# Three edits in a two-layer hybrid decoder step: order of the sample and mixing steps, and the last norm

## The chip, the core and the metric

The kernel runs on one core of a Trainium2 chip. The core has TensorE (PE: matrix products, with its weight loads shown apart as PEld), VectorE (DVE), ScalarE (ACT), GpSimd (POOL) and SyncE (SP), which here only issues DMAs. The time is the device time of one execution in microseconds; lower is better. PE's clock is granted by the chip: a granted clock of 1.00 is 2.4 GHz, and the share shown for a stretch (PEclk) mixes that level with the one of 1.2 GHz.

## The reference

One inference step of a decoder trunk with two layers, for one prompt of 1024 tokens and eight samples of eight tokens (1088 rows of 1024 columns in all):

```python
def layer(x, past_kv, win_prev, wkv_prev, shift_prev, conv_prev, p):
    xn = rms_norm(x, p['norm_mix'])
    proj = xn @ p['w_in']
    ...
    o_nsa = nsa_attention(q, gates, kv_all, win_ext, p['cmp_pe'], p['cmp_w1'], p['cmp_w2'])
    o_rw, wkv_new, shift_new = rwkv_mixer(p_rw, shift_prev, wkv_prev, p)
    x = x + jnp.concatenate([o_nsa, o_rw], axis=-1) @ p['w_out']
    f, conv_new = conv_ffn(rms_norm(x, p['norm_ffn']), conv_prev, p)
    return x + f, ...
```

`nsa_attention` has three branches for 8 query heads and 2 key heads: compressed blocks of keys, the 8 blocks of 64 keys with the highest compressed scores ("selected"), and a sliding window of 256; sigmoid gates weigh and add the three. `rwkv_mixer` is a delta-rule recurrence over the tokens with 8 heads of 64, followed by a group norm, a bonus term and a gate. After the last layer `rms_norm(x, norm_final)` gives the outputs; `rms_norm` divides each row by the root of its mean square plus 1e-6 and multiplies by a gain per column.

## The kernel before

Activations lie transposed: 128 of the 1024 columns on the partitions, the 1088 tokens along the free axis. Each layer runs four stages, one after the other:

- `projections`, 0 to 377 us (layer 0) and 2130 to 2499 (layer 1);
- `scan_with_samples`, 377 to 918 and 2499 to 3041: the RWKV recurrence of the prompt, with the attention of the eight samples laid between its steps;
- `prompt_mixing`, 918 to 1241 and 3041 to 3369: the prompt's attention and the end of the RWKV branch;
- `dense_layer`, 1241 to 2130 and 3369 to 4282: output projection, ConvFFN and, in the last layer, the final norm.

Inside a stage each engine has generators of steps, written out by hand: `scan_tensor` beside `sample_tensor` on PE, `scan_vector` beside `sample_vector` on DVE, and so on. One function interleaves them alike on every engine, so the program order is fixed, and semaphores alone tie the engines together; an engine that waits holds up everything behind it in its own order.

**Scan stage.** `turns()` (L877) takes one scan step, then a sample step when its share is due. There are 152 scan steps, 19 for each pair of chunks of 64 tokens: Gram products, their masked turn, the start values, then five times a "y" step (L1284, 32 records of products in the trace) and a "z" step (L1297 and L1298, 64 records; L1298 alone in the last of the five), then "p" (L1306), "u" (L1313) and "state" (L1320, L1329, L1330) steps for both chunks. The products' results are added on DVE (L1430 for y and z, L1442 for the state). There are 143 sample steps, 16 for each of eight groups (one sample each) and a short closing group. On PE a group goes: the hidden layer of the key compression (L1504, in eight half-products of eight records each, one step each), scores, the importance product L1561 with the transposes of the compressed and window weights, then the products of window and compressed values ("w_out", L1571 to L1578), then the transposes of the selected weights:

```python
m.then_inc(w_out, 1)
yield
pe.wait_ge(s_exp, c + 1)
for n in range(8):
    pe.transpose(ps[:, BA + n * 64:BA + n * 64 + 64], s_[:, n * P:(n + 1) * P], ...)
```

(L1583), and the product with the selected values (L1591). In the same steps DVE ranks the 17 blocks (`block_ranks`, L1864 to L1872), masks the scores by the choice (L1743 to L1746), and finds the row maximum (to L1749); ACT then takes the exponential (L1648), which sets s_exp. A product c_made closes each group's compressed keys, and the last scan step's output is what the first RWKV loads of the next stage (ro_ga, waited for at L2340) come after.

**Mixing stage.** `blend()` (L1963) interleaves three generators on every engine: `compressed` (56 steps, seven per tile of 128 queries), `output` (the RWKV branch's group norm, bonus and gate, 43 steps) and `attention` (87 steps over 80 pieces of up to four key tiles). In each of its 87 rounds it takes a compressed step (two in the first six), then an output step when due, then the attention step. On DVE an attention step masks the scores of piece i+4 (L2162, L2165) and then forms the factors of a finished row of pieces i+2 ("scale", the reciprocal L2180 and the gate L2182, 128x2 each). On POOL `norm` (L2199) multiplies the exponentials by those factors, and PE transposes them (L2089) in the step after. POOL's compressed steps are the subtraction of the maximum (L2284), the gating `cm_sg` (L2290, asked for by PE's transposes L2221) and the counts (L2296, L2299); its output steps are `weigh(j)`: four operations of 128x512 on one token tile (L2455, L2457, L2458, L2459), all in one step, every third output step.

**Last norm.** At the end of `dense_layer` of the last layer DVE has the sums of squares per column-group in `rs` (128 x 1088). `sums()` (L2610) multiplies them by a matrix of ones, so every partition gets the sum of each token; `factor()` scales the 1088 sums (L2698), ACT takes the root (L2670) and DVE the reciprocal (L2701), all on 128x1088; eight multiplications (L2735) and their stores end the kernel.

## Time and profile before

| | us |
|---|---|
| median of three runs | 4283.41 (4283.08 to 4290.14) |
| the profiled execution | 4283.59 |
| its span in the trace | 4281.8 |
| PE busy | 3987.7 |
| DVE, POOL, ACT busy | 2198.1, 1785.7, 1121.3 |

The profile is of one execution. "Busy" is the time with an instruction of that engine running; a row that ends in [3.29 <-ACT sa_s L1648] says that the engine had been idle for 3.29 us and that the write of sa_s at L1648 ended it. PEclk is the granted clock of PE, as a share of the full one. The time of the profiled execution is 1.8 us above its span and 0.2 us from the median.

### The profile page before, as it was taken

The numbers are of one execution on the slowest core, as the hardware profiler recorded it, in microseconds if no ns is written. First come the engines' busy times: TensorE is split into PE (matmuls) and PEld (weight loads), VectorE is DVE, ScalarE is ACT, GpSimd is POOL, SyncE is SP. The second block draws the span as 40 slices with busy tenths as digits, with TensorE's granted clock in tenths as the row PEclk, the third lists the DMA queues.
The fourth block names the chain that finished last, engine by engine and source line by source line (L and its number), as shares of the span: only waits on it lengthen the run. The fifth ranks groups of instructions, "written<-read, shape, count | busy, mean of one in ns | idle before, by whom it ended". The sixth has DMA issues, their size and how long they took to land. (4 is left out here: it accounts for less than half of the span.)

```text
span 4281.8 us, 89487 instructions
## 1 busy us (share of the span) xinstructions
PE 3987.7 (93%) x37002; PEld 3633.0 (85%) x37002; DVE 2198.1 (51%) x4923; ACT 1121.3 (26%) x2467; POOL 1785.7 (42%) x2332
## 2 busy tenths in 40 slices
PE   8998999978899999999999979999888999999997
PEld 8987888865579999999899868888655799999996
DVE  6686444458754423414456864434587445244153
ACT  3153232326551100000212523233355410000011
POOL 5532212127765444434355322122377644344342
PEclk9999999979999999999999999999799999999998
DMA  3254323220012122131323452232200221311312
GB/s 132 91 158 163 97 72 81 67 90 6 12 54 104 45 96 77 45 125 46 112 85 117 135 176 76 67 79 66 90 9 10 75 92 45 108 66 45 129 40 89
DMA packets 201960, 350.42 MB, mean 82 GB/s; under 512 B 72930, under 2 KB 135650, under 8 KB 200418
## 3 DMA queue, kind: packets, MB, share of 16 engines
q1 hardware_dynamic: 201554, 344.70, 25.5%
q8 instruction: 293, 4.80, 0.5%
q14 instruction: 113, 0.93, 0.1%
HBM read 253.44 MB, written 95.90 MB: 82 GB/s over the span
## 5 line engine op out<-in xcount | busy, mean ns | idle before, releaser
L2601 POOL CAST wr_hi<-wr_raw 128x256 fp32r<-128x256 f32 x584 | 264.7, 453 | 902.8 <-PE ps L2636 897.1
L2603 POOL TENSOR_TENSOR wr_lo<-wr_raw,wr_hi 128x256 fp32r<-128x256 f32 x584 | 548.4, 939 | 46.8
L2636 PE MATMUL ps<-xh,wr_hi 128*128 128x384 f32 x2064 | 453.4, 328 | 0.0
L2636 PE MATMUL ps<-xl,wr_hi 128*128 128x384 f32 x2064 | 453.1, 327 | 0.0
L2636 PE MATMUL ps<-xh,wr_lo 128*128 128x384 f32 x2064 | 453.1, 327 | 0.0
L1377 POOL TENSOR_TENSOR rc_CT<-rc_AT,rc_masks 128x256 f32<-128x256 f32 x192 | 138.4, 741 | 665.1 <-DVE rc_AT L1412 486.4
L2636 PEld LDWEIGHTS ps<-xh,wr_hi 128*128 128x128 f32 x2064 | 349.2, 188 | 0.3
L2636 PEld LDWEIGHTS ps<-xh,wr_lo 128*128 128x128 f32 x2064 | 348.8, 188 | 0.0
L2636 PEld LDWEIGHTS ps<-xl,wr_hi 128*128 128x128 f32 x2064 | 348.7, 188 | 0.0
L2674 ACT ACTIVATE de_c<-de_c 128x1088 f32<-128x1088 f32 (+1 forms) x44 | 49.1, 1115 | 1098.4 <-DVE de_c L2761 1098.4
L2636 PE MATMUL ps<-de_mixh,wr_hi 128*128 128x384 f32 (+3 forms) x1440 | 320.8, 331 | 7.9 <-DVE de_mixl L2708 7.9
L2636 PE MATMUL ps<-de_mixl,wr_hi 128*128 128x384 f32 (+3 forms) x1440 | 318.4, 329 | 0.0
L2636 PE MATMUL ps<-de_mixh,wr_lo 128*128 128x384 f32 (+3 forms) x1440 | 317.4, 329 | 0.0
L2199 POOL TENSOR_TENSOR at_s<-at_s,at_fac 128x384 f32<-128x384 f32 (+3 forms) x320 | 256.2, 827 | 139.8 <-DVE at_fac L2182 139.0
L2722 DVE TENSOR_TENSOR de_x<-de_x,ps 128x384 f32<-128x384 f32 x168 | 79.3, 528 | 454.0 <-PE ps L2636 454.0
L1504 PE MATMUL ps<-sa_kt,cp_w 128*128 128x126 f32 x2304 | 295.2, 281 | 0.0
L1504 PEld LDWEIGHTS ps<-sa_kt,cp_w 128*128 128x128 f32 x2304 | 268.0, 191 | 9.7
L2636 PEld LDWEIGHTS ps<-de_mixh,wr_hi 128*128 128x128 f32 (+1 forms) x1440 | 245.4, 189 | 14.9 <-issue 14.9
L2636 PEld LDWEIGHTS ps<-de_mixh,wr_lo 128*128 128x128 f32 (+1 forms) x1440 | 247.4, 188 | 0.0
L2636 PEld LDWEIGHTS ps<-de_mixl,wr_hi 128*128 128x128 f32 (+1 forms) x1440 | 243.5, 188 | 0.0
L520 PE MATMUL ps<-pr_wh,xh 128*128 128x256 f32 (+1 forms) x720 | 215.7, 300 | 2.7 <-ACT pr_rsm L696 2.7
L520 PE MATMUL ps<-pr_wl,xh 128*128 128x256 f32 (+1 forms) x720 | 207.8, 289 | 0.0
(450 smaller groups left out, 8359.4 us busy)
## 6 DMA issues: line engine op xcount, KB each, us to landing
sa_kvp<-in_cache SPq DMA_DIRECT2D x128, 256.0 KB
scr_xres<-de_x SPq DMA_DIRECT2D x56, 544.0 KB, 2.7
de_x<-scr_xres SPq DMA_DIRECT2D x56, 544.0 KB, 3.6
wr_raw<-in_w_gate SPq DMA_DIRECT2D x42, 512.0 KB, 3.5
wr_raw<-in_w_up SPq DMA_DIRECT2D x42, 512.0 KB, 3.5
rc_arbk<-scr_arbk SPq DMA_DIRECT2D x32, 512.0 KB, 4.8
wr_raw<-in_w_down SPq DMA_DIRECT2D x32, 512.0 KB, 3.6
pr_raw<-in_w_rw SPq DMA_DIRECT2D x28, 512.0 KB, 4.3
```

Source lines behind the costliest of these rows:

```text
L520: mm = pe.matmul(ps[0:m, b:b + w], x[:, k, t * P:t * P + m], weights(y, i)[:, k, :], start=(k == 0 and j == 0), stop=(k == KD - 1 and j == 2))
L1377: pool.tensor_tensor(CT[:, n % 2, s], AT[:, s], mid(lev[:, n * CH:(n + 1) * CH], 4), ALU.mult).then_inc(ct_ready[s], 1)
L1504: m = pe.matmul(ps[:, b:b + 126], w1[:, kv, q, half * P:(half + 1) * P], kt[:, 2 * kv:2 * kv + 2, q % 8, q // 8:q // 8 + 63], start=(q == ...
L2199: pool.tensor_tensor(x, x, fac[:, job % 6, g:g + 1].to_broadcast([P, w]), ALU.mult).then_inc(normed, 1)
L2601: pool.tensor_copy(hi[:, k, :], raw[:, k, :]).then_inc(w_hi, 1)
L2603: pool.tensor_tensor(lo[:, k, :], raw[:, k, :], f32(hi[:, k, :]), ALU.subtract).then_inc(w_ready, 1)
L2636: m = pe.matmul(ps[:, (bank + b) * BANK:(bank + b) * BANK + cols], w[rows, k, :], x[rows, k, o:o + cols], start=(k == 0 and i == 0), stop= ...
L2674: act.activation(c[rows, :], c[rows, :], ACT.Silu).then_inc(silu_done, 1)
L2722: m = dve.tensor_tensor(to[:, o:o + w], x[:, o:o + w], ps[:, (bank + b) * BANK:(bank + b) * BANK + w], ALU.add)
```

## The change

Three edits that don't touch one another.

**Scan stage.** On PE the second half-product of the first half of L1504's sum and the first one of the second half go in one step (six hidden steps a group instead of eight), and two empty steps come between the w_out products and the transposes of the selected weights. ACT has the same two empty steps ahead of its exponential. On DVE `block_ranks` is split: the comparisons (`block_orders`) stay, the ranks go one step later, the masks one more, and one empty step follows them. The waiting counts on SP and POOL follow, and the closing group has 9 steps in place of 11. SAMPLE_STEPS goes from 143 to 141.

```diff
@@ sample_tensor
-                            yield
+                            if (half, part) != (0, 1):
+                                yield
...
                 m.then_inc(w_out, 1)
                 yield
+                yield
+                yield
                 pe.wait_ge(s_exp, c + 1)
@@ sample_scalar
                 act.copy(pwT[0:8, 2, :], ps[0:8, BC + 128:BC + 192]).then_inc(p_copied, 1)
+                yield
+                yield
                 yield
                 act.wait_ge(s_masked, c + 1)
@@ sample_vector
-                step(block_ranks(dve, step, sel[:, :, :], im2, 64, 1, 17, K["low17"], gt, eq, rank))
+                block_orders(dve, step, im2, 64, 1, 17, gt, eq)
+                yield
+                step(block_ranks(dve, step, sel[:, :, :], 64, 1, 17, K["low17"], gt, eq, rank))
                 yield
...
                 dve.tensor_scalar(st[:, 12:13], st[:, 11:12], st[:, 10:11], -SCALE, ALU.max, ALU.mult).then_inc(s_masked, 1)
+                yield
                 yield
```

PE in the sixth sample group of layer 0, before; rc_ tiles are the scan's, sa_ tiles the samples', and L1583 the transposes of the selected weights:

```order
L1561 MATMUL ps<-sa_im,sa_cm 64x17
L1563 MATMUL ps<-cbuf,sa_pg 64x64
L1565 MATMUL ps<-cbuf,sa_s 128x64 x2
L1566 MATMUL ps<-cbuf,sa_s 8x64
L1284 MATMUL ps<-rc_XX,rc_CT 64x64 x16
L1571 MATMUL ps<-sa_vc,sa_pT 32x64 x2
L1576 MATMUL ps<-sa_wk,sa_pT 32x64 x4
L1578 MATMUL ps<-sa_wn,sa_pT 32x64 x2
L1298 MATMUL ps<-rc_XX,rc_ys 64x64 x16
L1583 MATMUL ps<-cbuf,sa_s 128x64 x8
L1584 MATMUL ps<-cbuf,sa_s 8x64
L1306 MATMUL ps<-rc_S,rc_arbk 64x64 x8
```

and in the changed kernel, from the same w_out products on (L1572 is the old L1571, L1586 the old L1583, L1594 the old L1591):

```order
L1572 MATMUL ps<-sa_vc,sa_pT 32x64 x2
L1577 MATMUL ps<-sa_wk,sa_pT 32x64 x4
L1579 MATMUL ps<-sa_wn,sa_pT 32x64 x2
L1284 MATMUL ps<-rc_XX,rc_CT 64x64 x16
L1298 MATMUL ps<-rc_XX,rc_ys 64x64 x16
L1306 MATMUL ps<-rc_S,rc_arbk 64x64 x8
L1586 MATMUL ps<-cbuf,sa_s 128x64 x8
L1587 MATMUL ps<-cbuf,sa_s 8x64
L1313 MATMUL ps<-rc_p_64,rc_XX 64x64 x8
L1594 MATMUL ps<-sa_kvp_4773,sa_pT 32x64 x16
```

Between w_out (to L1578) and the transposes stood one z step, the last of its five; now the last y step, the last z step and a p step stand there. The product with the selected values comes one scan step behind the transposes, as before.

**Mixing stage.** On DVE and POOL the attention step of a round is taken first, ahead of the compressed and the output step; PE, ACT and SP keep their order. In DVE's attention step `scale` comes before `mask`. `weigh(j)` is cut in three parts, taken in three consecutive output steps.

```diff
@@ blend(attention, compressed, output, first=False)
     for i in range(ATTENTION_STEPS):
+        if first:
+            next(attention)
         for _ in range(2 if i < 6 else 1):
...
-        next(attention)
+        if not first:
+            next(attention)
@@ attention_vector
             for i in range(-LAG, NI + 2):
+                if 0 <= i + 2 < NI and ITEMS[i + 2][7]:
+                    scale(i + 2)
                 if 0 <= i + 4 < NI:
                     mask(i + 4)
-                if 0 <= i + 2 < NI and ITEMS[i + 2][7]:
-                    scale(i + 2)
                 yield
@@ output_pool
             for j in range(TT):
-                if j + 1 < TT:
-                    weigh(j + 1)
-                yield
-                yield
-                yield
+                for part in range(3):
+                    if j + 1 < TT:
+                        weigh(j + 1, part)
+                    yield
```

The parts are: 0 the product with the bonus; 1 the product with the norm's gain; 2 the norm's offset and the sum. POOL in mixing of layer 0, before (at_s is attention, cm_ the compressed branch, ro_ the output branch):

```order
L2199 TENSOR_TENSOR at_s<-at_s,at_fac 128x384 x2
L2290 TENSOR_TENSOR cm_sg<-cm_s,gate 128x512
L2455 TENSOR_TENSOR ro_v_13702<-ro_v_13702,ro_bonus 128x512
L2457 TENSOR_TENSOR ro_y<-ro_y,ro_gn_13704 128x512
L2458 TENSOR_TENSOR ro_y<-ro_y,ro_gn_13704 128x512
L2459 TENSOR_TENSOR ro_y<-ro_y,ro_v_13702 128x512
L2199 TENSOR_TENSOR at_s<-at_s,at_fac 128x512 x2
L2199 TENSOR_TENSOR at_s<-at_s,at_fac 128x384 x2
L2296 TENSOR_TENSOR cm_eq<-cm_eq,cm_const 128x256 x2
L2299 TENSOR_TENSOR cm_gt<-cm_gt,cm_eq 128x512
```

and in the changed kernel, the same place (L2216 is the old L2199; L2480, L2470, L2473 and L2474 are the four operations of `weigh`):

```order
L2307 TENSOR_TENSOR cm_sg<-cm_s,gate 128x512
L2216 TENSOR_TENSOR at_s<-at_s,at_fac 128x512 x2
L2216 TENSOR_TENSOR at_s<-at_s,at_fac 128x384 x2
L2480 TENSOR_TENSOR ro_v_13702<-ro_v_13702,ro_bonus 128x512
L2216 TENSOR_TENSOR at_s<-at_s,at_fac 128x384 x2
L2313 TENSOR_TENSOR cm_eq<-cm_eq,cm_const 128x256 x2
L2316 TENSOR_TENSOR cm_gt<-cm_gt,cm_eq 128x512
L2216 TENSOR_TENSOR at_s<-at_s,at_fac 128x384 x2
L2470 TENSOR_TENSOR ro_y<-ro_y,ro_gn_13704 128x512
L2216 TENSOR_TENSOR at_s<-at_s,at_fac 128x384 x4
L2301 TENSOR_TENSOR cm_s<-cm_s,cm_m_110 128x512
L2473 TENSOR_TENSOR ro_y<-ro_y,ro_gn_13704 128x512
```

The four `weigh` operations stood in one piece ahead of four normalisations; now normalisations stand between the pieces.

**Last norm.** The sums of squares go through nine column products (`rs` as the stationary side, one column of ones), which leave the 1088 sums as 128 x 9; scaling, root and reciprocal run on those, nine products of 128x128 with the identity spread each column back over the partitions, and three copies bring them from PSUM to `rs`. The root's table is asked for by a root of one column ahead of the last square.

```diff
@@ dense_layer, PE, end
-                sums()
+                for t in range(TT):
+                    w = min(P, NT - t * P)
+                    m = pe.matmul(ps[0:w, 7 * BANK + 400 + t:7 * BANK + 401 + t], rs[:, t * P:t * P + w], cst["ones"][:, 0:1], start=True, stop=True)
+                m.then_inc(summed, 1)
+                pe.wait_ge(rs_ready, 2)
+                for t in range(TT):
+                    w = min(P, NT - t * P)
+                    o = (5 + t // 3) * BANK + t % 3 * P
+                    m = pe.matmul(ps[:, o:o + w], r9[0:w, t:t + 1].to_broadcast([w, P]), cst["ident"][0:w, 0:w], start=True, stop=True)
+                m.then_inc(spread, 1)
@@ ACT, end
-                        act.activation(rs[:, :], rs[:, :], ACT.Sqrt).then_inc(rooted, 1)
+                        act.activation(r9[:, :], r9[:, :], ACT.Sqrt).then_inc(rooted, 1)
+                        act.wait_ge(spread, 1)
+                        act.copy(rs[:, 384:768], ps[:, 6 * BANK:6 * BANK + 384])
+                        act.copy(rs[:, 768:NT], ps[:, 7 * BANK:7 * BANK + 320]).then_inc(copied, 1)
```

DVE's last rows before:

```order
L2692 TENSOR_TENSOR rs<-rs,de_h 128x1088
L2698 TENSOR_SCALAR rs<-ps 128x384 x2
L2698 TENSOR_SCALAR rs<-ps 128x320
L2701 RECIPROCAL rs<-rs 128x1088
L2735 SCALAR_TENSOR_TENSOR de_xf_44509<-de_xf_44509,de_gn,rs 128x1088 x8
```

and in the changed kernel:

```order
L2729 TENSOR_TENSOR rs<-rs,de_h 128x1088
L2773 TENSOR_SCALAR de_r_273<-ps 128x8
L2774 TENSOR_SCALAR de_r_273<-ps 64x1
L2776 RECIPROCAL de_r_273<-de_r_273 128x9
L2778 COPY rs<-ps 128x384
L2781 SCALAR_TENSOR_TENSOR de_xf_44528<-de_xf_44528,de_gn,rs 128x1088 x8
```

Three scalings and a reciprocal over all 1088 columns become two scalings and a reciprocal over nine columns and one copy; the eight closing multiplications are the same.

## Rows read from the trace of the kernel before

**Rows 1.** Windows by stage; columns: window, us, busy us of each engine (records), PEclk, DMA, GB/s:

```profile
376.80:918.00 541.20, 496.83 (x8924) 442.30 (x8924) 232.68 (x612) 150.81 (x352) 115.18 (x159) 0.94 0.32 91
918.00:1241.00 323.00, 269.41 (x2023) 177.65 (x2023) 240.01 (x729) 185.49 (x517) 216.69 (x239) 0.89 0.09 28
1241.00:2130.00 889.00, 881.13 (x5292) 875.02 (x5290) 358.94 (x542) 98.75 (x101) 397.19 (x590) 1.00 0.25 83
2499.00:3041.00 542.00, 493.10 (x8918) 437.90 (x8916) 232.98 (x612) 151.04 (x352) 116.88 (x160) 0.95 0.31 90
3041.00:3369.00 328.00, 271.69 (x2050) 177.44 (x2050) 241.74 (x733) 188.33 (x530) 218.71 (x245) 0.90 0.08 27
```

**Rows 2.** PE's waits: line, engine and line waited for, us in total, times, longest:

```profile
PE ps L2089 <- POOL at_s L2199: 55.6, 36, 6.5
PE ps L1583 <- ACT sa_s L1648: 32.9, 13, 3.3
...
PE ps L2340 <- DMA ro_ga<-scr_xmT: 13.2, 2, 6.8
...
PE ps L2221 <- POOL cm_sg L2290: 6.3, 2, 3.2
```

**Rows 3.** Windows of the stretches around L1583 in layer 0, and their sum:

```profile
486.00:501.00 15.00, 11.71 (x237) 10.59 (x232) 7.86 (x24) 3.63 (x9) 0.15 (x1) 0.77 0.06 18
...
591.00:606.00 15.00, 11.67 (x283) 9.91 (x283) 11.43 (x33) 6.26 (x17) 7.37 (x10) 1.00 0.39 107
646.00:656.00 10.00, 8.12 (x116) 7.14 (x117) 6.86 (x24) 2.35 (x6) 0.00 (x0) 0.66 0.06 15
...
756.00:771.00 15.00, 11.66 (x250) 10.18 (x244) 10.06 (x32) 4.09 (x11) 0.00 (x0) 0.89 0.01 3
...
sum 115.00, PE 89.88 PEld 79.42 DVE 70.82 ACT 31.19 POOL 13.93; mean PE 11.23 PEld 9.93 DVE 8.85 ACT 3.90 POOL 1.74
```

**Rows 4.** Timeline of the first sample group, layer 0: start us, us, instruction, idle before it:

```profile
483.47 1.25 PE L1284 MATMUL ps<-rc_XX,rc_CT 64*64 64x64 f32 x32
...
487.67 0.68 DVE L1743 CUSTOM_DVE_ANT_1 sa_s<-ps,sa_sel 64x512 f32<-64x512 f32 x1
...
489.57 1.16 ACT L1648 ACTIVATE sa_s<-sa_s,sa_st 64x1032 f32<-64x1032 f32 x1 [4.45 <-DVE sa_st L1749]
...
490.88 1.11 PE L1583 MATMUL ps<-cbuf,sa_s 64*128 64x64 f32 x8 [3.29 <-ACT sa_s L1648]
...
492.02 1.97 PE L1284 MATMUL ps<-rc_XX,rc_CT 64*64 64x64 f32 x32
```

**Rows 5.** Windows of the mixing stage of layer 0:

```profile
956.00:1026.00 70.00, 63.42 (x543) 44.16 (x540) 61.00 (x173) 49.08 (x119) 47.42 (x51) 0.98 0.00 1
1026.00:1151.00 125.00, 96.39 (x704) 62.01 (x700) 99.91 (x262) 65.29 (x184) 91.89 (x96) 0.88 0.05 14
1151.00:1241.00 90.00, 83.36 (x692) 54.39 (x691) 50.27 (x218) 59.83 (x190) 58.75 (x74) 1.00 0.01 3
```

**Rows 6.** Timeline inside the middle stretch, GpSimd and PE:

```profile
1036.17 1.04 POOL L2290 TENSOR_TENSOR cm_sg<-cm_s,gate 128x512 f32<-128x512 f32 x1
...
1044.10 4.15 POOL L2199 TENSOR_TENSOR at_s<-at_s,at_fac 128x512 f32<-128x512 f32 x4
...
1045.37 2.29 PE L2089 MATMUL ps<-cbuf,at_s 128*128 128x128 f32 x8 [3.71 <-POOL at_s L2199]
```

**Rows 7.** One line's instructions, L2182: duration ns min/median/max, first and last start:

```profile
L2182 DVE TENSOR_TENSOR at_fac<-at_fac,gate x128: 160/161/2016, 939.4 to 3364.9; 128x2 f32<-128x2 f32 x128
```

**Rows 8.** Timelines: the last norm, and products of the new norm's shapes elsewhere:

```profile
914.38 2.04 PE L2215 MATMUL ps<-kcz,qT 128*128 128x128 f32 x8 [5.42 <-PEq L169]
...
2136.18 2.05 PE L578 MATMUL ps<-cbuf,rs 128*128 128x1 f32 x18
...
4253.48 4.00 PE L2610 MATMUL ps<-rs,cbuf 128*128 128x384 f32 x6 [4.04 <-DVE rs L2692]
...
4260.11 6.95 DVE L2701 RECIPROCAL rs<-rs 128x1088 f32<-128x1088 f32 x1 [1.18 <-ACT rs L2670]
```

More of the change, by code:

```diff
@@ L871 @@
 SCAN_STEPS = 19 * PAIRS
-SAMPLE_STEPS = 4 + 16 * NB + 11
+SAMPLE_STEPS = 4 + 16 * NB + 9
 LEAD = 10
@@ L1460, in sample_sync @@
                     load_rows(sp, c + 1)
-                for n in range(11):
+                for n in range(9):
                     yield
@@ L1467, in sample_sync @@
                     return
-                for n in range(4):
+                for n in range(6):
                     yield
@@ L1698, in sample_vector @@
                     yield
-                for n in range(8):
+                for n in range(6):
                     if c == 0 and n == 1:
@@ L1785, in sample_pool @@
             for c in range(NB + 1):
-                for n in range(11):
+                for n in range(9):
                     yield
@@ L1789, in sample_pool @@
                     return
-                for n in range(5):
+                for n in range(7):
                     if n == 0:
@@ L1866, in block_ranks @@
     step(m)
+def block_ranks(dve, step, sel, rows, g, nb, low, gt, eq, rank):
+    lo = low[0:rows].rearrange("p (s t) -> p s t", s=nb).unsqueeze(1).to_broadcast([rows, g, nb, nb])
     for n in range(g):
@@ L1960, with blend @@
 ATTENTION_STEPS = len(ITEMS) + LAG + 2
-def blend(attention, compressed, output):
+def blend(attention, compressed, output, first=False):
     done_c = done_o = 0
     for i in range(ATTENTION_STEPS):
+        if first:
+            next(attention)
+            assert not 1 <= i <= len(ITEMS) or done_c >= 7 * (T_ORDER.index(ITEMS[i - 1][0]) + 1) or ITEMS[i - 1][2]
         for _ in range(2 if i < 6 else 1):
```

48 lines of the change are left out of this document (33 added, 15 removed).

## The prediction

> **What bounds the kernel now.** I read the page first, where TensorE (PE) is by far the busiest engine, then the windows by stage [rows 1]. The dense stage leaves it 8 of 889 us at full clock, so nothing outside its last microseconds can be had there. The scan stage leaves 44.4 of 541.2 us idle at a granted clock of 0.94, the mixing stage 53.6 of 323.0 us at 0.89; the second layer's two stages read alike (48.9 us at 0.95, 56.3 us at 0.90). So a change in these two stages counts twice. Third, the list of PE's waits [rows 2]: the largest is mixing's L2089 on GpSimd's normalisation L2199 (55.6 us, 36 times), the second L1583, the transposes of the selected weights, on the exponential L1648 (32.9 us). These are what parts B and A aim at. In both stages a microsecond of PE idle costs more than itself when the clock falls with it, so I count both: idle, and (1 − granted clock) times the length.
>
> **A, the selected transposes.** The eight stretches around L1583 in layer 0 hold 115 us, of which PE is busy 89.88: 25.1 us idle [rows 3]. Their clock is 0.77 in three, 1.00 in one, 0.66 in one (10 us long), 0.89 in three: 3 × 3.45 + 3.4 + 3 × 1.65 = 18.7 us lost. In the first group [rows 4] masks run on DVE from 487.67, the exponential starts at 489.57, and PE, which had one scan step behind w_out, waits 3.29 us until 490.88. The y step L1284 takes 1.25 us before the wait and 1.97 after it: that is the clock term in two rows.
>
> Now three scan steps instead of one stand between w_out and the transposes. They are not free cover: each has its own hand-offs on DVE, queued behind ranks and masks (masks 1.9 us from 487.67 to the exponential). I laid the new order out by hand with the traced durations (y 1.25, z with twice its products about 2.0, masks 1.9, exponential 1.3 to its release); laid out the same way, the old order gives 2.9 us where the trace has 3.29. For the first group three steps of 1.25 + 2.0 + 1.25 = 4.5 us stand there; the exponential is hidden but for 0.2 us, and the second y step waits 1.5 us, since the z adds come behind the masks: 1.7 remain. The eight groups, by the scan steps that they meet: 1.7, 1.2, 3.2, 2.3, 3.0, 2.4, 1.2, 1.7 = 16.7 us, against 25.1 idle: 8.4 us gained. The waits become several of 1 to 1.5 us instead of one of 3.3. What the clock does with that no row shows for sure: [rows 3] has one stretch at 1.00 with 3.3 us idle and one at 0.66 with 1.9 us idle. The loss may stay at 18.7 or go to nothing; I take half, 9.3 us, since three of eight stretches already stand at 0.89 with the same idle. A = 2 × (8.4 + 9.3) = 35 us; ends 2 × (8.4 − 4) = 9 (waits as long as before in half of the groups, clock unchanged) and 2 × (8.4 + 18.7) = 54.
>
> Ends of the stage: at its start PE's first wait for the samples' rows has one scan step more before it: −1 a layer. At its end PE's closing c_made product stands ahead of the last scan step, so that the last scan output, and after it the DMA of ro_ga for which L2340 waits up to 6.8 us already [rows 2], come later by that product: +1. I let them cancel. The merged products L1504 and the empty steps issue nothing new; the DMAs keep their order on SP.
>
> **B, attention first in mixing.** The middle stretch, 1026 to 1151, is where the stage loses: PE 96.39 of 125 busy at clock 0.88, so 28.6 idle and 15 us of clock, with DVE 99.9 and GpSimd 91.9 busy; its last 90 us have 83.36 busy at 1.00 [rows 5]. The loss comes in spikes, one per token tile: GpSimd takes L2290 at 1036.17 and then all four operations of weigh, 1037.2 to 1044.1, before it gets to the normalisation L2199, for which PE waits 3.71 us [rows 6]. After the change L2199 comes first in each step and weigh in three pieces, so that the norm waits at most for a piece that already runs (one to two of the four operations that now fill 6.9 us). But DVE's work stays at 99.9 us: that is the floor of the stretch, a gain of 25, and at the share at which the stretch before it runs DVE (61.00 of 70, 87% [rows 5]) it takes 99.9 / 0.87 = 115, a gain of 10. I take 15, nearer to the second. The rest of the stage, less dense, gives 4.
>
> Against it: the compressed branch's hand-offs now queue behind attention. GpSimd's norm (four instructions, 4.15 us [rows 6]) can stand ahead of L2290 (1.04 us), for which PE's L2221 asks, and ahead of the subtraction for the exponential, and PE's own order is not changed. By the timeline's slack most of this is hidden: 4 us per layer, and 1 at the start. B = 2 × (15 + 4 − 4 − 1) = 28 us. Ends: −12, with hand-offs of 24 us a layer in place of 4, and +50, with 25 a layer.
>
> The same tiny DVE instruction L2182 has a median of 161 ns and a maximum of 2016 ns [rows 7]; the long ones run beside GpSimd's tensor operations. So part of DVE's 99.9 us is time blocked by GpSimd, and the change, which leaves the same work on both, gets that time back only if overlaps happen to get rarer. The Trainium skill, page "SBUF — State Buffer", section "Who interferes with whom", has a rule for this: a VectorE instruction with two SBUF inputs contends with a GpSimd one that reads SBUF, by an exclusive lock, and the one that issued first keeps it. The rows of L2182 agree (a 128x2 operation of up to 2016 ns). By that rule the work of weigh and norm would block DVE for the same total wherever it stands, and the kernel would come out at rival 2's time instead of the forecast.
>
> **C, the last norm.** From the end of the sum of squares to the eight closing multiplications the chain is 4253.48 to 4267.10, 13.6 us: six broadcast products 4.00, three scalings, a square root, and a reciprocal of 128x1088 of 6.95 us [rows 8]. All of it lies on the path that sets the end. New chain: nine column products (18 records for the same nine took 2.05 us at L578), two scalings of some 0.17 each with the hand-over 0.4, root 0.2, reciprocal 0.2, each with some 0.1 of hand-over, nine 128x128 spreads and three copies of about 0.5 (two on ScalarE in a row, 1.0). For the spreads, L2215's four such products (8 records) took 2.04 us at the low clock, so nine are 4.6; at full clock half. 2.05 + 0.4 + 0.3 + 0.3 + 4.4 + 1.0 ≈ 8.5 us. C = 5 us, 4 to 7.4 by the clock of the column products and the spreads. The table load stays where it is hidden. Everything before is the same work with the same weights.
>
> **The sum.** 35 + 28 + 5 = 68 us; the profiled execution took 4283.59, the median of the runs 4283.41, so both give about 4216. Two layers' worth of A and B is a sum of four stages; if one of them gives nothing, it is 4230 to 4235.
>
> **Rivals.** (1) The clock does not come back and the waits only move: A gives 2 × 8 = 16, time 4235. For it: the stretch at 0.66 had just 1.9 us of idle [rows 3]. Against: the other low stretches each hold one wait over 3 us. (2) B gives nothing, since DVE and GpSimd block each other for the same total as now and DVE is what mixing waits for: 4283.6 − 35 − 5 = 4243.6. For it: DVE busy 99.9 of 125 [rows 5] and the maximum of L2182 [rows 7]; against: the 3.71 us wait in [rows 6] is plainly for place in GpSimd's order. (3) More: the middle stretch of mixing falls to the level of the last one (83.36 of 90 at 1.00 [rows 5]), 44 us × about 0.5 a layer; B = 44 to 50 and A at its end of 54: 4175 to 4181. (4) Slower: PE, which still takes compressed work ahead of attention, waits for the two late hand-offs of each query tile. Norm's 4.15 us less about 1.4 us of slack is 2.75 us a hand-off; 2 × 8 tiles × 2 layers × 2.75 = 88 us, against A, B and C: 4283.6 − 68 + 88 ≈ 4303. It decides the sign when mixing grows by over 20 us a layer. Against it: L2221's waits are 6.3 us in two layers' 16 tiles in all [rows 2], so today there is slack. (5) The change doesn't do what it says: the order lists show that it does, so only C or nothing moves: 4278; I give it almost nothing.
>
> **How the numbers follow.** Forecast around 4216 (4200 to 4230) 0.4; rival 1 0.17; rival 2 0.15; rival 3 0.17; both 1 and 2 together (4262 to 4265) 0.05; slower 0.04; no change 0.02. A measurement of this kernel can tell about 0.2%, 8.6 us, from no change. So faster by over that 0.93, within it 0.03, slower 0.04. The range 4168 to 4260 leaves out rival 4, the pair of 1 and 2, and the far ends of 3.
>
> **What would show each step.** A: eight stretches around the select transposes with PE idle near 17 us a layer and clock mostly 0.9 or more; the wait L1583 for the exponential under 8 us in all, waits of the scan steps on DVE up by 10 to 20. B: PE's wait for the normalisation from 55.6 to some 25, mixing stages 309 and 314 us long; DVE busy unchanged. If L2221 or the compressed exponential's transposes show up with over 20 us of waits, rival 4 acts. C: closing chain 8 to 9 us and the first closing multiplication that much after the last sum. Wrong in all: if the scan stage is as long as before though its waits shrank, the clock took it; if mixing is as long with GpSimd's wait gone, DVE was the bound.

## The result

The changed kernel takes 4231.12 us (median of four runs, 4226.66 to 4235.38) against 4284.03 for the kernel before in the same session: ratio 0.9873, 95% interval 0.9856 to 0.9891. It is 53 us faster in the medians; the profiled execution (4226.66 us, span 4224.9) is 57 us under the one of before. One of the ten executions of e2 below was slow, 6403.12 us at a mean granted clock of 0.552, and no ratio counts it.

PE was busy for 3956.3 us in the changed kernel, for 3987.7 us before; the busy times of DVE, ACT and POOL differ by 5 us or less.

Where the 57 us went is best read by stages cut at the same instructions: the first Gram product of the scan, the first product of the compressed branch, and the first ConvFFN product. The windows of the changed kernel for the scan stages, cut so, and for the mixing stages, from their first product to about their last step, columns as in [rows 1]:

```profile
382.80:891.70 508.90, 477.18 (x8881) 426.50 (x8881) 228.95 (x600) 148.19 (x349) 115.52 (x159) 0.97 0.32 90
891.70:1216.00 324.30, 263.96 (x2046) 175.81 (x2048) 247.44 (x737) 186.11 (x527) 217.72 (x245) 0.91 0.10 32
2475.80:2986.40 510.60, 477.01 (x8881) 425.34 (x8881) 229.30 (x600) 148.17 (x349) 115.53 (x159) 0.98 0.32 90
2986.40:3313.00 326.60, 267.77 (x2058) 179.17 (x2058) 246.64 (x737) 187.31 (x530) 217.19 (x245) 0.90 0.10 32
```

and of the kernel before, layer 0, cut in the same way:

```profile
382.80:914.40 531.60, 490.68 (x8881) 437.19 (x8881) 227.81 (x600) 148.37 (x349) 115.18 (x159) 0.95 0.31 86
914.40:1241.00 326.60, 271.43 (x2031) 179.37 (x2031) 241.58 (x732) 186.71 (x518) 216.69 (x239) 0.89 0.10 32
```

The scan stage went from 531.6 to 508.9 us: PE's busy time fell by 13.5 us with the same 8881 records, which is clock (0.95 to 0.97), and its idle time by 9.2, from 40.9 to 31.7. From the first mixing product to the first ConvFFN product (the start of the dense stage included) both layers gained little: 431.5 to 428.1 and 431.7 to 429.2. The end gained 3.8. So A brought 22.7 + 23.1 = 45.8 us, B 3.4 + 2.5 = 5.9, C 3.8; the last 1.5 us lie between the stages named. B's 5.9 us are no more than such a stage varies by from run to run (see the table below), so B's gain can hardly be told from nothing by these numbers.

PE's waits in the changed kernel, to be held against [rows 2]; L2238 is the old L2221, L2088 the old L2071, L2106 the old L2089, L1586 the old L1583:

```profile
PE ps L2238 <- POOL cm_sg L2307: 48.7, 14, 8.3
PE ps L2088 <- DVE at_mx L2179: 22.9, 16, 4.6
...
PE ps L1313 <- DVE rc_p L1436: 10.5, 6, 5.2
...
PE ps L2088 <- DVE at_mx L2182: 8.8, 7, 1.6
...
PE ps L1586 <- ACT sa_s L1654: 7.4, 8, 2.0
...
PE ps L2106 <- POOL at_s L2216: 0.8, 2, 0.4
PE ps L1493 <- POOL sa_kvc L1785: 0.8, 1, 0.8
```

The two waits at which the change aims are much shorter: the normalisation from 55.6 to 0.8 us, the exponential from 32.9 to 7.4. The scan's own waits on VectorE (rc_XX, rc_p and rc_UV together) came up by 13.4 us, and in mixing a wait of 48.7 us for cm_sg stands where 6.3 stood: the gating of the compressed branch is now late. The scores' waits for the masks (at_mx) went from 20.4 to 31.7 us, and those of L2106 for at_pT from 0.8 to 8.8.

In mixing the changes of these four waits add up to 7 us more of waiting, not less. PE's idle time from the first mixing product to the first ConvFFN product grew, from 59.5 to 64.3 us and from 60.9 to 62.8; what made the stages 3.4 and 2.5 us shorter is PE's busy time for the same records, 372.0 to 363.8 and 370.9 to 366.4 us, at a granted clock of 0.93 and 0.92 where 0.91 and 0.92 stood.

The stretches around the selected transposes of layer 0, eight of 15 us, against [rows 3]:

```profile
485.00:500.00 15.00, 14.08 (x341) 12.84 (x338) 9.38 (x28) 5.34 (x12) 1.41 (x2) 1.00 0.11 25
...
639.00:654.00 15.00, 14.29 (x285) 12.52 (x283) 8.39 (x23) 6.29 (x14) 5.89 (x9) 0.84 0.15 34
...
745.00:760.00 15.00, 13.00 (x250) 11.62 (x245) 8.91 (x30) 5.54 (x11) 0.00 (x0) 0.89 0.09 17
...
sum 120.00, PE 109.02 PEld 98.31 DVE 74.18 ACT 44.66 POOL 21.81; mean PE 13.63 PEld 12.29 DVE 9.27 ACT 5.58 POOL 2.73
```

Six of the eight have the full clock; the two below it are shown. PE is busy 109.02 of 120 us: 11.0 idle in place of 25.1 of 115, and (1 − 0.84) and (1 − 0.89) of 15 us, 4 us of clock in place of 18.7. The first group, against [rows 4]:

```profile
484.79 1.15 PE L1284 MATMUL ps<-rc_XX,rc_CT 64*64 64x64 f32 x32
...
488.29 1.16 ACT L1654 ACTIVATE sa_s<-sa_s,sa_st 64x1032 f32<-64x1032 f32 x1 [1.93 <-DVE sa_st L1757]
...
488.99 1.28 PE L1284 MATMUL ps<-rc_XX,rc_CT 64*64 64x64 f32 x32 [0.92 <-DVE rc_XX L1430]
...
490.20 0.71 PE L1586 MATMUL ps<-cbuf,sa_s 64*128 64x64 f32 x8
```

The transposes come without a wait. The exponential ran while PE waited for the second y step's input and then took that step, which waited 0.92 us for the z additions behind the masks, and nothing runs at the low clock.

In mixing one late gating looks like this (POOL and DVE of the changed kernel; L2216 is the normalisation, L2474 the last operation of weigh, L2278 the probabilities on VectorE, L2307 the gating cm_sg):

```profile
1012.56 4.07 POOL L2216 TENSOR_TENSOR at_s<-at_s,at_fac 128x512 f32<-128x512 f32 x4 [0.51 <-DVE at_fac L2199]
...
1020.38 0.69 DVE L2278 TENSOR_TENSOR cm_s<-cm_s,cm_m 128x512 f32<-128x512 f32 x1
1020.39 1.79 POOL L2474 TENSOR_TENSOR ro_y<-ro_y,ro_v 128x512 f32<-128x512 f32 x1
...
1022.15 1.04 POOL L2307 TENSOR_TENSOR cm_sg<-cm_s,gate 128x512 f32<-128x512 f32 x1
...
1023.24 1.12 PE L2238 MATMUL ps<-cbuf,cm_sg 128*128 128x128 f32 x4 [5.20 <-POOL cm_sg L2307]
```

PE waits 5.20 us for L2307. Two things stand ahead of it: VectorE finishes the probabilities only at 1021.07, behind attention's factors and masks of the same round, and GpSimd comes to the gating behind a normalisation of 4.07 us and the pieces of weigh, which had collected behind it and run here one after the other, with no normalisation between them.

Of the 16 gatings only this one and its like in the second layer start when GpSimd is through with earlier work. The other 14 start 0.1 us after VectorE's probabilities, on a GpSimd that stands idle (us in total, times):

```profile
  DVE cm_s L2278: 29.2, 14
```

The longest of PE's waits for cm_sg, 8.3 us until 930.1, is of this kind. VectorE stood idle for 3.01 us ahead of the attention's factors, which wait for ScalarE's exponential, with the compressed work behind them:

```profile
925.22 0.17 DVE L2197 RECIPROCAL at_fac<-at_sm 128x2 f32<-128x2 f32 x1 [3.01 <-ACT at_s L2142]
```

So in the changed kernel the gating is late for the most part by VectorE's order.

The closing chain, against [rows 8]:

```profile
4198.94 1.29 DVE L2729 TENSOR_TENSOR rs<-rs,de_h 128x1088 f32<-128x1088 f32 x1 [1.18 <-ACT de_h L2698]
...
4200.28 3.74 PE L2665 MATMUL ps<-cbuf,rs 128*128 128x1 f32 x18 [4.04 <-DVE rs L2729]
...
4204.82 4.40 PE L2671 MATMUL ps<-cbuf,de_r 128*128 128x128 f32 x18 [0.81 <-DVE de_r L2776]
...
4210.10 10.19 DVE L2781 SCALAR_TENSOR_TENSOR de_xf<-de_xf,de_gn,rs 128x1088 f32<-128x1088 f32 x8 [0.28 <-ACT rs L2707]
```

From the last sum of squares to the first closing multiplication it is 9.87 us, where 13.6 stood.

### The profile page after: what moved, and what is told of

It is laid out like the page before. It is cut to its first block and busy times, and to the rows that moved or that the text cites. A ratio compares the mean times of both kernels' runs of the same rounds, so it can differ in the third digit from the quotient of the medians.

```text
span 4224.9 us, 89599 instructions
## 1 busy us (share of the span) xinstructions
PE 3956.3 (94%) x37032; PEld 3618.4 (86%) x37032; DVE 2200.1 (52%) x4925; ACT 1116.3 (26%) x2470; POOL 1781.1 (42%) x2332
## 5 line engine op out<-in xcount | busy, mean ns | idle before, releaser
L2625 POOL TENSOR_TENSOR wr_lo<-wr_raw,wr_hi 128x256 fp32r<-128x256 f32 x584 | 548.7, 940 | 46.7
L2216 POOL TENSOR_TENSOR at_s<-at_s,at_fac 128x384 f32<-128x384 f32 (+3 forms) x320 | 251.3, 811 | 96.2 <-DVE at_fac L2199 93.1
L1504 PE MATMUL ps<-sa_kt,cp_w 128*128 128x126 f32 x2304 | 285.8, 280 | 0.0
L1504 PEld LDWEIGHTS ps<-sa_kt,cp_w 128*128 128x128 f32 x2304 | 265.4, 192 | 7.3
```

Source lines behind the costliest of these rows:

```text
L1504: m = pe.matmul(ps[:, b:b + 126], w1[:, kv, q, half * P:(half + 1) * P], kt[:, 2 * kv:2 * kv + 2, q % 8, q // 8:q // 8 + 63], start=(q == ...
L2216: pool.tensor_tensor(x, x, fac[:, job % 6, g:g + 1].to_broadcast([P, w]), ALU.mult).then_inc(normed, 1)
L2625: pool.tensor_tensor(lo[:, k, :], raw[:, k, :], f32(hi[:, k, :]), ALU.subtract).then_inc(w_ready, 1)
```

## The experiments

Stage lengths of all runs, between the instructions named above, layer 0 / layer 1 in us:

| kernel | median, ratio with 95% interval | scan | mixing to first ConvFFN product |
|---|---|---|---|
| before | 4284.03 | 531.6 / 533.7 | 431.5 / 431.7 |
| changed | 4231.12, 0.9873 (0.9856 to 0.9891) | 508.9 / 510.6 | 428.1 / 429.2 |
| e1 scan edit alone | 4236.99, 0.9879 (0.9855 to 0.9903) | 507.9 / 509.8 | 432.2 / 432.5 |
| e2 empties at the end | 4305.88, 1.0046 (1.0034 to 1.0059) | 540.7 / 546.9 | 428.8 / 433.9 |
| e3 masks and exponential early | 4292.05, 1.0012 (1.0001 to 1.0023) | 536.1 / 543.5 | 429.3 / 435.1 |
| e8 masks early, exponential late | 4262.76, 0.9939 (0.9924 to 0.9954) | 519.3 / 523.9 | 431.9 / 433.6 |
| e4 weigh in pieces alone | 4263.75, 0.9949 (0.9930 to 0.9968) | 529.9 / 536.3 | 423.5 / 420.1 |
| e5 changed, attention last | 4214.26, 0.9829 (0.9815 to 0.9842) | 510.0 / 512.4 | 420.9 / 418.6 |
| e6 the same, factors first | 4207.61, 0.9810 (0.9794 to 0.9826) | 507.9 / 512.6 | 416.9 / 416.9 |
| e7 attention first on VectorE alone | 4258.10, 0.9930 (0.9915 to 0.9945) | 509.7 / 510.7 | 441.7 / 445.1 |
| e9 attention first on GpSimd alone | 4247.23, 0.9907 (0.9889 to 0.9925) | 511.2 / 513.8 | 437.2 / 436.2 |
| e10 e6 with less weigh | 4203.39, 0.9806 (0.9781 to 0.9830) | 512.2 / 511.3 | 415.9 / 415.5 |
| e11 attention ahead of output | 4216.33, 0.9831 (0.9805 to 0.9857) | 508.4 / 512.6 | 422.3 / 419.7 |
| e12 e6 with filler products | 4202.05, 0.9801 (0.9787 to 0.9814) | 509.5 / 510.5 | 417.4 / 417.0 |

Each ratio is against runs of the kernel before on the same chip, whose medians lay at 4284 to 4289 us; e10 rests on two executions. Stages of the same order differ by up to 4.3 us from run to run: the nine kernels with the changed scan have scan stages of 507.9 to 512.2 and 509.8 to 513.8 us, the five with the old mixing order have 428.8 to 432.2 and 431.7 to 435.1. That is the error to be kept in mind in these columns.

### e1: the scan edit alone

The diff is the scan part of the change and nothing else.

> The kernel before with the scan-stage edit alone. If the three edits add up stage by stage (theory 1), it takes what the two scan stages lost between the two traces, 22.6 + 23.0 = 46 us: 4284 - 46 = 4238, mixing stages 431.5 us from their first product to the first ConvFFN product as before. If the edits help each other through the clock or the DMAs (rival), it stays 10 us or more above that, 4248 or more.

Measured 4236.99, with scan stages of 507.9 and 509.8 us. The edits add up by stage; nothing of A's gain needs B or C. The mixing stages are 432.2 and 432.5 us, as before.

### e2: the empty steps at the end of the group

```diff
@@ sample_tensor, against e1 (ACT, DVE and SP alike; ranks and masks as in the kernel before)
                 m.then_inc(w_out, 1)
                 yield
-                yield
-                yield
                 pe.wait_ge(s_exp, c + 1)
...
                 m.then_inc(s_out, 1)
                 yield
+                yield
+                yield
```

> The scan-stage edit alone, but the two empty steps stand behind the product with the selected values, at the end of each group, on every engine, and the ranks and masks stand where they stood before: the transposes again come one scan step behind w_out. Merged products, step counts and starts are as in e1. Cover theory: the wait of the transposes for the exponential is back at about 33 us in all, the clock losses too, and the gain is only what the start of the stage gives (PE's wait for sa_kvc, 11.1 us to 0.8): 4284 - 10 = 4274. Pace theory (the merged products and the earlier start do the work): 4240 to 4250, close to e1.

Measured 4305.88: slower than the kernel before, outside what either theory gave. PE's waits of e2:

```profile
PE ps L1586 <- ACT sa_s L1654: 43.5, 16, 4.0
...
PE ps L1313 <- DVE rc_p L1436: 20.2, 10, 5.1
```

All 16 groups now wait for the exponential (before, 13 waits of 32.9 us), and the "u" step waits 20.2 us for rc_p, which the list of before does not hold. Merging two products and shifting the group costs 9 and 13 us a layer by itself; against that, the cover together with the spreading of ranks and masks is worth 33 and 37 (e1 against e2). These two are the whole gain of A, and more than its gain; the pace theory is out. e3 and e8 take them apart.

### e3 and e8: ranks and masks in their old steps

```diff
@@ sample_vector, against e1, both
                 block_orders(dve, step, im2, 64, 1, 17, gt, eq)
-                yield
                 step(block_ranks(...))
...
                 dve.tensor_scalar(st[:, 12:13], ...).then_inc(s_masked, 1)
                 yield
                 yield
+                yield
@@ sample_scalar, against e1, e3 only
                 act.copy(pwT[0:8, 2, :], ...).then_inc(p_copied, 1)
                 yield
-                yield
-                yield
                 act.wait_ge(s_masked, c + 1)
                 act.activation(s_[:, :], s_[:, :], ACT.Exp, ...).then_inc(s_exp, 1)
                 yield
+                yield
+                yield
```

> The scan-stage edit alone, with PE's two empty steps where the change has them, but comparisons, ranks, masks and exponential in the steps in which they stood before (block_ranks in one piece, the two free steps behind the exponential). If cover for the exponential is all that counts, this is as good as e1 or better by the 7.4 us that L1583's successor still waits: 4231 to 4238. If the scan's own additions, queued behind ranks and masks on DVE in one piece, count as much (the reason for spreading them over three steps), PE's waits on DVE in the y, z, p and state steps grow by 1 us a group and more, 16 groups: 4254 or more.

> As e3 (scan-stage edit alone; comparisons, ranks and masks on VectorE in the steps in which they stood before, one piece), but ScalarE takes the exponential two steps later, as in the change. It splits e3's loss of 55 us against e1. If ScalarE's place is the reason (in e3 PE waited 34 us for ScalarE's copies of the scan, in e1 under 6): 4240 to 4252. If VectorE's one piece is the reason (19.2 us wait for rc_XX in e3 against 9.2): 4260 to 4290.

e3 took 4292.05, e8 4262.76, e1 4236.99. PE's waits of e3:

```profile
PE ps L1284 <- DVE rc_XX L1430: 19.2, 13, 3.4
...
PE ps L1297 <- ACT rc_ys L1359: 11.9, 4, 3.0
...
PE ps L1320 <- ACT rc_UV L1365: 10.1, 4, 2.6
```

The expectation for e8 set ScalarE's place against VectorE's one piece; its time lies in the range of the second, but both cost, and ScalarE's place the more. An exponential asked for early blocks ScalarE, which waits for the masks with the scan's copies (L1297 and L1320 wait for them) queued behind it; that costs 17 to 20 us a scan stage (e3 against e8). Ranks and comparisons in one piece, the masks a step earlier, make VectorE's additions late: 11 and 14 us a stage (e8 against e1). PE's wait for the exponential is small in both (2.8 us in e8), so cover in PE's order alone is worth little: of e1's 33 and 37 us over e2, PE's two steps bring 5 and 3 (e3), ScalarE's 17 and 20, the spreading on VectorE 11 and 14.

### e4: weigh in pieces alone

The diff is the `weigh(j, part)` part of the change, on the kernel before.

> The kernel before with weigh in three pieces alone; attention stays last on every engine, factors after the mask. Theory 1 (queue place): the normalisation no longer stands behind four operations, so PE's wait for it drops from 55.6 to about 30 us, but the pieces now stand ahead of the gating cm_sg: its waits go up from 6.3 to 20 to 30; 4270 to 4284. Rival (VectorE and GpSimd block each other, the order does nothing): 4284 with both waits changed but the mixing stages at 431 to 432 us.

Measured 4263.75, better than expected by either. PE's waits in it:

```profile
PE ps L2089 <- POOL at_s L2199: 28.7, 37, 3.3
PE ps L2071 <- DVE at_mx L2162: 21.9, 18, 2.9
...
PE ps L2221 <- POOL cm_sg L2290: 6.3, 2, 3.2
```

The normalisation's wait halved, and the gating's did not rise at all; the masks' waits (L2162 and L2165) went from 20.4 to 33.1 us, about what they are in the changed kernel. Of B's three parts this one alone brings 8 and 12 us a layer, more than all of B.

### e5 and e6: the changed kernel with attention last

```diff
@@ against the changed kernel; blend() takes the order of a round as letters
-            blend(attention_vector(dve), compressed_vector(dve), output_vector(dve), first=True)
+            blend(attention_vector(dve), compressed_vector(dve), output_vector(dve), order="COA")
...
-            blend(attention_pool(pool), compressed_pool(pool), output_pool(pool), first=True)
+            blend(attention_pool(pool), compressed_pool(pool), output_pool(pool), order="COA")
@@ attention_vector, e5 only
-                if 0 <= i + 2 < NI and ITEMS[i + 2][7]:
-                    scale(i + 2)
                 if 0 <= i + 4 < NI:
                     mask(i + 4)
+                if 0 <= i + 2 < NI and ITEMS[i + 2][7]:
+                    scale(i + 2)
```

> The changed kernel, but on VectorE and GpSimd the attention step comes last in a round again and the factors after the mask, as before the change; weigh stays in three pieces. If attention-first is what gave back the gain of the pieces (theory 1: the wait for cm_sg 48.7 us in the changed kernel, 6.3 in e4), the mixing stages take what they take in e4 and the kernel is some 16 us faster than the changed one: 4231 - 16 = 4215. If the pieces' gain in e4 was only to be had with the old scan stage (rival), it stays at 4231.

> As e5, but the factors of attention (scale) stay ahead of the mask, as in the change: the one small edit of VectorE's order alone. Theory 1: the normalisation starts up to two masks (about 1.2 us) earlier, of its wait of 28.7 us in e4 10 to 15 go, and the masks come that much later, so the scores' wait for at_mx rises by about as much: within 5 us of e5, 4210 to 4218. Rival (the factors' place is the part of the change that costs): 4222 or more.

e5 took 4214.26 where 4215 was expected, so close only by chance: attention first and factors first together give back 7 and 11 us a layer. e6 took 4207.61; its interval overlaps that of e5, but its mixing stages are 4.0 and 1.7 us shorter, which is within the repeat error of a stage. Against the changed kernel e6 differs in the order of the rounds alone, and its mixing stages are 11 and 12 us shorter: that is what attention first costs. Its waits:

```profile
PE ps L2086 <- DVE at_mx L2177: 32.6, 22, 3.2
...
PE ps L2086 <- DVE at_mx L2180: 19.5, 15, 2.8
...
PE ps L2104 <- POOL at_s L2214: 7.7, 12, 2.0
...
PE ps L2236 <- POOL cm_sg L2305: 4.6, 2, 2.3
```

Factors ahead of masks take the normalisation's wait from 27.8 us (e5) to 7.7 and put 18 us on the scores' wait for the masks (33.9 to 52.1; L2177 and L2180 together): a wait that mostly moved.

### e7, e9 and e11: which engine's order is it

```diff
@@ e7: against the changed kernel; e9: against e6; e11: against the changed kernel
-            ... output_pool(pool), first=True)        (e7)
+            ... output_pool(pool), order="COA")
...
-            ... output_pool(pool), order="COA")       (e9)
+            ... output_pool(pool), order="ACO")
...
-            ... first=True)                           (e11, VectorE and GpSimd)
+            ... order="CAO")
```

> The changed kernel with GpSimd's rounds in the old order (compressed, output, attention) and VectorE's with attention first. Theory 1a (GpSimd's queue makes cm_sg late): the wait for cm_sg falls from 48.7 to under 15 us and the kernel is 10 us or more faster than the changed one, 4221 or less. Theory 1b (VectorE makes it late, since it forms the probabilities behind the attention's mask): the wait for cm_sg stays over 35 us, and the normalisation's wait comes back beside it: 4231 to 4245.

> e6 with attention first on GpSimd alone (VectorE keeps compressed, output, attention). Theory 1b (VectorE's late probabilities make cm_sg late, GpSimd's order does little): the wait for cm_sg stays under 15 us and the kernel is within 5 us of e6's 4208. Theory 1a (GpSimd's queue makes it late: a normalisation of 4 us ahead of the gating): the wait for cm_sg rises to 30 us or more and the kernel goes to 4218 or more.

> The changed kernel with the rounds of VectorE and GpSimd in the order compressed, attention, output (factors ahead of the mask, weigh in three pieces). It keeps the one thing that attention-first was to bring, no weigh piece ahead of a normalisation, without putting the compressed hand-offs behind attention. Theory 1 (late compressed hand-offs were the whole loss): cm_sg's wait under 10 us, kernel at e6's level or up to 6 us better, 4202 to 4210. Rival (output's own hand-offs also suffer when they come last, PE's wait on the output branch grows): 4215 or more.

Waits of e7, then of e9:

```profile
PE ps L2104 <- POOL at_s L2214: 46.7, 27, 5.6
PE ps L2236 <- POOL cm_sg L2305: 34.6, 12, 8.1
```

```profile
PE ps L2236 <- POOL cm_sg L2305: 36.5, 10, 9.6
...
PE ps L2104 <- POOL at_s L2214: 0.8, 2, 0.4
```

Attention first on VectorE alone makes the gating 34.6 us late, on GpSimd alone 36.5; each is enough. Both together (48.7) are not their sum, which fits a chain that runs through both: probabilities on VectorE, gating on GpSimd. In e9 12 of the 16 gatings start only when GpSimd is through with earlier work, where 2 did in the changed kernel; in e7 it is 2 again. e7's wait is as theory 1b said within 0.4 us, but its time lies 13 us over the range given; e9 came out as theory 1a said. Both kernels are slower than the changed one, by 27 and 16 us in the medians. In e7 the normalisation's wait is back at 46.7, behind compressed and output work on GpSimd, beside the late gating; in e9 it is 0.8 as in the changed kernel, and its masks' waits are 56.0 against 31.7. Most of the 16 us by which its mixing stages are longer is clock: PE's idle time in them is only 1.5 and 3.3 us above the changed kernel's, its busy time for the same records 7.6 and 3.7 us, at a granted clock of 0.90 against 0.93 and 0.92. Why the clock is lower there with nearly the same idle time is open. e11 keeps the compressed work ahead and puts attention before output only: the gating's wait is 11.5 us and the normalisation's 6.8. It comes out at 4216.33 (4203.73 to 4222.43), outside the expectation and at the rival's edge, with mixing stages 5 and 3 us longer than e6's. The rival's mechanism does not show: PE's idle time in the two stages is 52.8 and 53.3 us, in e6 53.6 and 51.5, and in the first of them the whole difference is busy time. So the late compressed hand-offs were most of the loss, and putting attention ahead of output work bought nothing once weigh was in pieces.

### e10: two of weigh's operations left out

```diff
@@ weigh(j, part), against e6
-                    step(pool.tensor_tensor(yj, yj, gn[0:n, 0, :], ALU.mult))
...
-                    step(pool.tensor_tensor(yj, yj, gn[0:n, 1, :], ALU.add))
```

> e6 with two of weigh's four operations left out (the group norm's gain and offset are not applied), so GpSimd has about 2 x 9 x 2 operations of 1.0 to 1.3 us less, some 21 us a layer in the mixing stage. Contention theory (VectorE is blocked by GpSimd's reads and is what the stage waits for): the mixing stages get 10 us or more shorter than e6's 416.9 each and VectorE's busy time there drops by as much. Queue-place theory (what counts is what stands ahead of the normalisation, and that is cured in e6): under 5 us a stage.

The kernel leaves out the group norm's gain and offset, so its outputs are not the model's; it serves for timing alone. Window of the mixing stage of layer 0, first of e6, then of e10 (columns as in [rows 1]):

```profile
890.30:1205.00 314.70, 265.02 (x2050) 176.26 (x2050) 249.31 (x737) 187.06 (x528) 216.11 (x245) 0.92 0.10 33
```

```profile
894.90:1209.00 314.10, 266.74 (x2052) 177.66 (x2054) 240.41 (x737) 187.87 (x530) 192.26 (x227) 0.91 0.10 33
```

GpSimd's busy time falls by 23.9 us and VectorE's by 8.9 for the same work: the blocking is real, 0.37 us of VectorE for each microsecond of such work. Most of the 8.9 us, 7.3, is in one line, the attention's factors times the gate (128x2, both inputs in SBUF). Here the Trainium skill's page "SBUF — State Buffer", section "Who interferes with whom", agrees with the trace as far as it goes: two-input VectorE operations and GpSimd reads get in each other's way. But the stages are only 1.0 and 1.4 us shorter, less than they vary from run to run: VectorE's busy share is not what they wait for. The contention theory of B (rival 2) is out for this stage as it stands in e6.

### e12: filler products ahead of the last norm

```diff
@@ dense_layer, PE, against e6
             if last:
+                for n in range(20):
+                    pe.matmul(ps[:, 6 * BANK:6 * BANK + P], cst["ident"], cst["ident"], start=True, stop=True)
                 pe.wait_ge(acc_done, 2 * (KD - 1))
...
                 m.then_inc(summed, 1)
+                for n in range(3):
+                    pe.matmul(ps[:, 6 * BANK:6 * BANK + P], cst["ident"], cst["ident"], start=True, stop=True)
                 pe.wait_ge(rs_ready, 2)
```

> e6 with 20 filler products of 128x128 (identity by identity, into a bank that the spread overwrites) between the last ConvFFN product and the column products of the last norm, and three more between the column products and the spreads; their results are not used. Clock theory for the missed term of C (the column products took 3.74 us at a granted clock of 0.53, the spreads 4.40 at 0.50, while eighteen such records took 2.05 at 1.00 in the kernel before): the two groups take about 2.05 and 2.2 us, and the chain from the last sum of squares to the first closing multiplication shrinks from 9.8 to 6 to 7 us; the kernel, 3 us less than e6, 4205. Rival (the products of this place are slow for another reason, their shape or operand): 3.7 and 4.4 us again, chain 9.8 or, with the fillers in the way, more.

What it tests shows in the granted clock of the two product groups of the changed kernel:

```profile
4200.20:4204.10 3.90, 3.74 (x18) 3.64 (x18) 0.07 (x2) 0.00 (x0) 0.00 (x0) 0.53 0.00 0
4204.80:4209.20 4.40, 4.38 (x18) 3.99 (x18) 0.00 (x0) 0.00 (x0) 0.00 (x0) 0.50 0.00 0
```

against that of L578 in the kernel before, from whose row I had the price:

```profile
2136.00:2138.20 2.20, 2.20 (x20) 2.05 (x18) 0.00 (x0) 0.00 (x0) 0.22 (x1) 1.00 0.99 318
```

The end of e12 (L2661 are the fillers, L2665 the columns, L2673 the spreads, L2783 the closing multiplications):

```profile
4174.67 4.73 PE L2661 MATMUL ps<-cbuf 128*128 128x128 f32 x40
...
4177.44 1.29 DVE L2731 TENSOR_TENSOR rs<-rs,de_h 128x1088 f32<-128x1088 f32 x1 [1.18 <-ACT de_h L2700]
...
4179.23 2.05 PE L2665 MATMUL ps<-cbuf,rs 128*128 128x1 f32 x18
...
4182.09 2.41 PE L2673 MATMUL ps<-cbuf,de_r 128*128 128x128 f32 x18
...
4185.38 10.19 DVE L2783 SCALAR_TENSOR_TENSOR de_xf<-de_xf,de_gn,rs 128x1088 f32<-128x1088 f32 x8 [0.28 <-ACT rs L2709]
```

The granted clock of the two groups in e12:

```profile
4179.20:4181.30 2.10, 2.10 (x21) 2.07 (x20) 0.00 (x0) 0.00 (x0) 0.00 (x0) 1.00 0.03 8
4182.00:4184.50 2.50, 2.50 (x20) 2.15 (x18) 0.04 (x1) 0.00 (x0) 0.00 (x0) 1.00 0.00 0
```

The columns take 2.05 us in place of 3.87 in e6, the spreads 2.41 in place of 4.40, both at 1.00 where e6 has 0.50. The last sum of squares ends at 4178.73, so the chain is 6.65 us against 10.0 in e6, as the clock theory said. At 4202.05 us this is the fastest kernel of the case, 29 us under the changed one in the medians and 0.9801 (0.9787 to 0.9814) of the one before; against e6 the chain's 3.4 us are shown by the trace, the rest of the 5.6 us between the medians is within their spread.

## Why the prediction held, point by point

**The time.** 4216 was forecast with 4168 to 4260; it is 4231. The sign and the range held; the sum was 68 us, the span moved by 57. That the sum came so near is in part luck: A was 11 us too low and B 22 us too high.

**A: the mechanism held, the size was 11 us low.** Forecast 35 us with ends of 9 and 54, measured 45.8. The exponential's wait is 7.4 us in all where under 8 was named. The idle term was 8.4 us a layer by the hand layout and is 9.2 and 11.8. In the eight stretches themselves PE is idle for 11.0 us where 16.7 were laid out, 14.1 less than before; about 5 us of that came back outside them. In the first group the second y step waits 0.92 us where 1.5 was laid out, the sixth waits 1.99 for its exponential where the layout had 2.4 in all. The clock term, for which half of 18.7 was taken for want of a row, is 13.5 and 11.3 us a layer: with waits of one to two microseconds in place of one of 3.3, six of the eight stretches have the full clock, before one had. The ends of the stage came to nothing, as forecast, but not by the terms named (1 us less at the start, 1 more at the end): at the start the wait for sa_kvc went from 11.1 to 0.8 us, and the "u" step behind it now waits for rc_p (4.1 and 5.2 us, 10.5 with its later waits); at the end PE's wait for ro_ga stayed (13.2, now 13.0). Rival 1 (waits move, clock stays low, 4235) has the time nearly right and its reason wrong.

**B: the term that was mis-sized.** Forecast 28 us, measured 5.9. The failed step is "by the timeline's slack most of this is hidden: 4 us per layer" for the late hand-offs of the compressed branch. They added 21 us a layer to PE's wait for cm_sg, and the stages are 11 and 12 us longer by them (e6 against the changed kernel). The slack that I read was that of the old order; each of the two moves uses it up alone (e7, e9). The gain side was there: the normalisation's wait fell by 55 us, where 30 were named. But half of that was to be had from weigh in pieces alone (e4), with the gating's wait as before. I had priced the pieces and attention-first as one edit; e4 shows that the pieces bring 8 and 12 us a layer, e6 that attention first takes 11 and 12 back. Without it, e6's mixing stages are 14.6 and 14.8 us shorter than before the change, what the forecast's 14 a layer named for the whole of B. One reading of [rows 6] was also off: of the 6.9 us from 1037.2 to 1044.1 the four operations of weigh fill 5.0, and for 1.82 us GpSimd stands idle between the first and the second, waiting for VectorE's ro_y; with weigh in pieces such a wait need not hold up a normalisation. Rival 4 (late hand-offs) was the true mechanism, at about half of its price of 2.75 us for each of 32 hand-offs when counted in PE's wait (48.7 − 6.3 = 42 us of 88), and at a quarter when counted in time (the 11 and 12 us); I had thought of it as all or nothing, at a chance of 4%, and it acted in part. What would show it, over 20 us of waits at L2221, was named, and it shows.

**C: one price at the wrong clock.** Forecast 5 us (4 to 7.4), measured 3.8, a chain of 9.87 us where 8 to 9 was named. The column products were priced from L578, whose 2.05 us stand at a granted clock of 1.00, while PE comes to the last norm after 4 us of idle, at 0.53: 3.74 us. With both groups at the low clock the forecast's own terms give 8.5 + 2 = 10.5 us, a gain of 3, so its lower end of 4 did not follow from them. The spreads were priced at the low clock and took 4.40 as laid out. e12 shows the column products at 2.05.

**DVE as the floor.** The 115 us for the middle stretch came from VectorE's busy share. In e6's order, e10 takes 9 us of VectorE's busy time away and the stage keeps its length: there it is no floor. For the changed kernel's own order no run tests it. VectorE's busy time was to stay unchanged; in the windows above it rose from 241.6 to 247.4 us, and to 249.3 in e6, for about the same records.

## What to carry to other kernels

Moving a step ahead in an engine's order moves every other step of that engine back: list for each of them who waits for the result, and follow the chain through all the engines it passes, since slack that each hand-off has by itself is spent only once. Cutting a long block of low-priority work into pieces got the urgent work through without making the other branch's hand-offs late, and open steps between a producer and its consumer paid in full only when they were opened on all engines of the chain. A stage can get shorter while PE's idle time in it grows: read idle time and busy time for the same records apart. When the price of an operation is taken from a row elsewhere, take the granted clock of both places with it.

## What the runs showed of the hardware

TensorE's products after a wait of 4 us ran at or near the lower of its two levels (1.2 GHz; granted clock 0.53 and 0.50): nine column products took 3.74 and 3.87 us, and 2.05 at 1.00 with 20 filler products in the gap, which delayed them by 0.4 us. In the scan stage the same 8881 records took 490.7 us before and 477.2 after the long waits had been broken up. Beside 23.9 us more of GpSimd's 128x512 operations VectorE was busy for 8.9 us more with the same work, and the stage was longer by 1.0 us.
